# The second token tile's residual of the expert layers added by VectorE at the layer's end, in place of two identity products of TensorE in front of the experts

## The reference, cut to what matters

```
h = _layer_norm(DN_ALPHA * h + mix, ln_g[layer, 0], ln_b[layer, 0])
ffn = _grouped_moe(h, w_router, b_router, w_gu[layer], w_down[layer])
h = _layer_norm(DN_ALPHA * h + ffn, ln_g[layer, 1], ln_b[layer, 1])
```

## Time and profile before

| | us |
|---|---|
| median of 3 runs | 666.47 |
| the three runs | 663.47, 667.05, 666.47 |
| the profiled execution | 664.13 |
| its span, first to last instruction | 662.4 |

### The profile page before, as it was taken

The page is one execution under the profiler, slowest core; times in us unless marked ns, Lnnn a source line. Parts: engine busy times, 40 slices in busy tenths (PEclk is TensorE's granted clock), DMA queues, the critical chain, the costliest instruction groups (busy, mean ns, idle before and its releaser), DMA issues.

```text
span 662.4 us, 7170 instructions
## 1 busy us (share of the span) xinstructions
PE 643.2 (97%) x2750; PEld 287.1 (43%) x2750; DVE 293.9 (44%) x774; ACT 146.9 (22%) x331; POOL 18.6 (3%) x37
## 2 busy tenths in 40 slices
PE   6999999999999999999999999999999999999993
PEld 5854564564333333333334455556333333333331
DVE  0010303467435345254365346668444434435356
ACT  1030343231121121121222042333112021021122
POOL 2030200000000000000000000100000000000000
PEclk9999999999999999999999999999999999999998
DMA  8999926266999999999999980946999999999981
GB/s 302 387 404 348 425 114 229 88 223 232 421 421 421 421 421 422 421 421 421 421 416 413 421 366 25 368 149 240 409 410 420 422 421 419 422 421 421 420 363 64
DMA packets 41448, 231.43 MB, mean 349 GB/s; under 512 B 10170, under 2 KB 10170, under 8 KB 15811
## 3 DMA queue, kind: packets, MB, share of 16 engines
q1 hardware_dynamic: 36976, 230.72, 85.8%
q10 hardware_dynamic: 4434, 0.21, 0.5%
HBM read 229.87 MB, written 1.05 MB: 349 GB/s over the span
## 4 chain that ended last, share of the span: by engine, by line
PE 94%; DVE 3%; DMA 1%; ACT 1%; issue 0%; SPq 0%; DVEq 0%; ACTq 0%
PE pb L679 33%; PE pb L478 20%; PE pb L709 16%; PE pb L537 5%; PE pb L729 4%; PE pb L851 2%; PE pb L652 2%; PE pb L435 1%; PE pb L428 1%; PE pb L631 1%; PE pb L654 1%; PE pb L446 1%; DVE bufC L1466 1%; DMA ring<-in_w_in_a 1%; PE pb L891 1%; PE pb L595 1%
## 5 line engine op out<-in xcount | busy, mean ns | idle before, releaser
L478 PE MATMUL pb<-ring,hT 128*128 128x512 f32 x320 | 144.4, 597 | 0.1
L709 PE MATMUL pb<-ring,bufC 128*64 128x512 f32 x512 | 116.4, 596 | 0.9 <-DVE bufC L1466 0.9
L679 PE MATMUL pb<-ring,hT 128*64 128x512 f32 x512 | 113.5, 593 | 0.0
L679 PE MATMUL pb<-ring,bufB 128*64 128x512 f32 x480 | 106.4, 593 | 0.0
L1466 DVE STREAM_TRANSPOSE bufC<-bufC 32x128 f32<-32x128 f32 x256 | 103.0, 402 | 3.8
L1492 DVE COPY bufA<-pb 32x512 f32<-32x512 f32 x64 | 43.7, 682 | 118.1 <-PE pb L709 117.0
L478 PEld LDWEIGHTS pb<-ring,hT 128*128 128x128 f32 x320 | 58.4, 190 | 64.5 <-issue 62.5
L679 PEld LDWEIGHTS pb<-ring,hT 128*64 128x64 f32 x512 | 36.4, 137 | 71.5 <-issue 71.5
L709 PEld LDWEIGHTS pb<-ring,bufC 128*64 128x64 f32 x512 | 34.8, 137 | 68.1 <-issue 65.3
L679 PEld LDWEIGHTS pb<-ring,bufB 128*64 128x64 f32 x480 | 33.9, 137 | 67.2 <-issue 65.4
L1069 ACT ACTIVATE bufA<-pb 32x512 f32<-32x512 f32 x64 | 37.8, 590 | 111.1 <-PE pb L709 110.3
(11 more groups left out here) (246 smaller groups left out, 430.3 us busy)
## 6 DMA issues: line engine op xcount, KB each, us to landing
ring<-in_w_gu SPq DMA_DIRECT2D x124, 1024.0 KB, 20.9
ring<-in_w_down SPq DMA_DIRECT2D x64, 1024.0 KB, 20.4
ring<-in_w_in_a SPq DMA_DIRECT2D x11, 1024.0 KB, 18.5
ring<-in_w_out_a SPq DMA_DIRECT2D x4, 1024.0 KB, 20.9
ring<-in_w_q_b SPq DMA_DIRECT2D x4, 1024.0 KB, 23.2
ring<-in_w_out_b SPq DMA_DIRECT2D x4, 1024.0 KB, 24.2
bufA<-in_w_gu SPq DMA_DIRECT2D x2, 1024.0 KB, 6.1
hT<-in_w_gu SPq DMA_DIRECT2D x2, 1024.0 KB, 7.6
```

The lines of the kernel that those rows point to most:

```text
L478: last = mm(pb[bank][:, :], hT[:, k, t * P:(t + 1) * P], slot(i0 + k // 2)[0][:, k % 2, c * HALF:(c + 1) * HALF], start=k == 0, stop=k == ...
L679: last = mm(pb[0][c * 64:(c + 1) * 64, :].rearrange("p (a n) -> p a n", a=2), xe[m % 2][:, k, g * SLOTS:(g + 1) * SLOTS], w.rearrange("p ( ...
L709: last = mm(to[c * 64:(c + 1) * 64, :], heT[u == EXPERTS - 1][:, (2 * hf + j) * 64:(2 * hf + j + 1) * 64], w[:, j, c * HALF:(c + 1) * HALF ...
```

## The change

The two `seed` products of tile 1 are taken out of each of the two layers, half 0 behind `place(l, 1)` and half 1 behind `gate_up(0)`. The wait on `ln_ready` that stood in front of half 0 stays. Banks 6 and 7 now start with the first scatter of the layer (start=True for t = 1, m = 0). At the end of the layer VectorE computes `ALPHA * h + bank` for each half of tile 1 into `res`, waits for it (`link`), takes `bn_stats` from `res`, and reads `res` again in the step of line 1560. Tile 0 is as it was.

```diff
-                def seed(t, c):
+                def seed(c):
-                    pe.wait_ge(ln_ready, 2 * (2 * NT * l + t) + c + 1)
-                    mm(pb[4 + 2 * t + c][:, :], alpha_i[:, :], h[:, t, c * HALF:(c + 1) * HALF],
+                    pe.wait_ge(ln_ready, 2 * 2 * NT * l + c + 1)
+                    mm(pb[4 + c][:, :], alpha_i[:, :], h[:, 0, c * HALF:(c + 1) * HALF],
                        start=True, stop=False, skip_group_check=True)
...
-                                     ye[t][:, c * HALF:(c + 1) * HALF], start=False, stop=m == QUADS - 1,
+                                     ye[t][:, c * HALF:(c + 1) * HALF], start=t == 1 and m == 0, stop=m == QUADS - 1,
...
                 place(l, 1)
                 pe.wait_ge(ln_ready, 2 * (2 * NT * l + 1) + 2)
-                seed(1, 0)
                 gather(0, 1, 3)
                 gather(0, 3, 2)
                 gate_up(0)
-                seed(1, 1)
...
                 for c in range(2):
                     dve.wait_ge(mix_done, 4 * n + 2 * t + c + 1)
-                    link(V.bn_stats(ln[:, t, 6 * c:6 * c + 6], pb[4 + 2 * t + c][:, :]))
+                    cc = slice(c * HALF, (c + 1) * HALF)
+                    if t:
+                        link(V.scalar_tensor_tensor(out=res[:, t, cc], in0=h[:, t, cc], scalar=ALPHA,
+                                                    in1=pb[4 + 2 * t + c][:, :], op0=ALU.mult, op1=ALU.add))
+                    link(V.bn_stats(ln[:, t, 6 * c:6 * c + 6], res[:, t, cc] if t else pb[4 + c][:, :]))
...
-                    V.scalar_tensor_tensor(out=res[:, t, cc], in0=pb[4 + 2 * t + c][:, :], scalar=ln[:, t, 12:13],
+                    V.scalar_tensor_tensor(out=res[:, t, cc], in0=res[:, t, cc] if t else pb[4 + c][:, :], scalar=ln[:, t, 12:13],
                                            in1=ln_row[0][:, cc], op0=ALU.subtract, op1=ALU.mult)
```

More of the change, by code:

```diff
@@ L744, in moe @@
                 for c in range(2):
-                    seed(0, c)
+                    seed(c)
                 stay_awake(3, 1)
```

## The result

The changed kernel is slower: 669.95 us median (667.55 to 670.85, 13 runs) against 666.19 us (663.47 to 667.05, 13 runs), ratio 1.006 with a 95% interval of 1.0047 to 1.0074. The executions of either kernel fall into two groups some 2 us apart (before 5 around 664.1 and 8 around 666.6 us, changed 6 around 668.4 and 7 around 670.4), and group against group the changed kernel is 4.3 and 3.8 us slower. The profiled execution took 670.52 us, in the upper group; that of the kernel before, 664.13, was in the lower.

A forecast was written before the change was run, and what follows sets the result against it. TensorE's chain of products, 94% of the 662.4 us, bounds the kernel. The terms -0.62 + 1.45 + 1.45 = +2.28 us gave 666.4 us profiled and 668.7 us on the median, 0.34% slower; range 665.5 to 670.9.

The forecast's parts named there:

- rival C: Layer 0's end: longer TensorE idling before the K/V projection lets its clock fall; +4.5 us, time 670.9; chance 0.10.
- Transfers at nothing: Whole kernel: transfers end ahead of their use and shift with TensorE, so they were put at nothing.
- The products, -0.62 us: Tile 1's four removed TensorE products, both layers: half 0 gains 0.31 us per layer, half 1 gains 0; 0.62 in all.
- Rival A: Both layers: the four removed products count in full, 3.44 us gained, giving -0.54 us in all; chance 0.05.
- The additions, 1.45 us at each end: Both layers' ends: VectorE's two new multiply-adds per layer are paid in full, 1.45 us each end.
- rival B: Layer 0's end: the 1.45 us vanish in VectorE's free time before tile 1's transposition; sum +0.83, 667.3 us; chance 0.11.
- The SBUF source: VectorE's four operations reading SBUF instead of PSUM: rows show at most 2 ns gain, against a page's 65 ns each.
- The clock at nothing: Layer 0's end: the sum has no term for TensorE's clock falling while it idles 2.6 us before the projection.
- C's price: Clock fall at layer 0's end: half speed for 4.4 us, read from the kernel's start, costs 2.2 us.

The follow-up runs named there:

- e4: Against the kernel before, only the two tile 1 products per layer removed, VectorE's layer end as before (residual left out): 663.65 us, ratio 0.9987.
- e1: Changed kernel, but at layer 0's end ScalarE copies transposed tile 0 before taking tile 1's square root: 664.87 us, ratio 1.0005 to the kernel before.
- e2: Changed kernel plus two unread identity products on TensorE behind tile 0's transposition at layer 0's end: 666.54 us, ratio 1.0031 to the kernel before.
- e5: Kernel before with only VectorE's two multiply-adds per layer added, all TensorE products kept: 668.9 us, ratio 1.0076, 6 runs.
- e3: Changed kernel with half 1's product back behind gate and up, VectorE adding only half 0's residual: 667.88 us, ratio 1.0032 to the kernel before.
- e8: Kernel before with ScalarE's copies ahead of the root, half 0's product replacing an identity product, and line 550's four products split in pairs: 663.53 us, ratio 0.9982.

## Why the prediction was right in its range, and which term its sum lacked

The measured 669.95 us lies in the range of 665.5 to 670.9, on the side that was forecast, but beyond the forecast of 668.7 and slower by over 0.5%, to which I gave 0.23. The ends of the forecast's own terms reached only to 669.7: the result is inside because the range was stretched to rival C, to which I gave 0.10. Step by step:

- **Transfers at nothing**: right. From the first product of expert 1 to the start of the last scatter it is 181.95 us in both kernels in layer 0 (347.97 - 166.02 and 345.83 - 163.88).
- **The products, -0.62 us**: measured -0.55 by landmarks and 0.9987 in e4. In layer 0 half 1 gave 0.04 us (forecast 0) and half 0 gave 0.23 (forecast 0.31, ends 0.22 and 0.41): the gather's weight load came 0.12 us behind the table (155.91 - 155.79), where 0.05 us had been seen. Rival A is refuted by e4 and by both idle times.
- **The additions, 1.45 us at each end**: measured 1.43 and 1.44. Reading who is queued behind the square root was the step that counted: rival B, which looks only at tile 1's own users, would have given +0.83 us. e1 shows that another order of ScalarE, in two places, makes it true.
- **The SBUF source**: the rows were right to go by. The 65 ns per operation, estimated from the Trainium skill, "VectorE: DVE Perf Modes", section "The TRN2 errata — SBUF-src ops pay a fixed extra latency per instruction", did not show: with the source in SBUF `bn_stats` is 4 ns shorter and the step behind it 3 ns longer.
- **The clock at nothing is the step that failed.** The sum has no term for it; it stood only in rival C, and C is what happened. The trace of the changed kernel shows it, e2 and e5 tie it to the idle stretch, and the times say that it happens in all 13 runs: the lowest is 667.55 us, and the eight lower runs of e2, in which the clock stays up, lie from 666.26 to 666.61. The sentence that misled me is "An idle stretch of 2.6 us is shorter than that, which speaks against C". I took the 4.4 us between the last product and the fall at the kernel's end as a time that idling must last. But that fall shows only that 4.4 us are enough: I used an upper bound as a lower one. In the changed kernel the clock fell 2.2 us after the last product (356.04 to 358.2), before the projection had started.
- **C's price**, 2.2 us, was too high: 1.48 us in the trace, 1.70 in e5's, 1.9 from the medians of e2. I took it from the kernel's start, where half speed for 4.4 us was my own reading: the granted clock in both stretches of the earlier trace rows is 1.00. In layer 0's end the clock was low for 3.4 us, and TensorE had work in 3.0 of them.
- **Small slips**: on the highest run of before the forecast is 667.05 + 2.28 = 669.3 us, not 669.4.

Sum: -0.55 + 1.43 + 1.46 + 1.44 = +3.8 us. The forecast of +2.28 lacked the third term, the clock.

## What to carry to other kernels

A product that stands in front of a wait is filler; before moving its work to another engine, read who released the next instruction, and try first to put it where the engine waits anyway. When an engine gets more to do, follow each semaphore it sets to the engine that waits, and then read what is queued behind that wait: here nothing that reads the additions' result was late, but two copies queued behind a square root were. And count the idle time that a delay adds to TensorE: here 1.4 us more of it let the clock fall, which cost as much again. Put the next independent work into it, or, as in e2, two products that nobody reads.

## What the runs showed of the hardware that I had not expected

The granted clock falls after much less than the 4.4 us seen at the end of the kernel. In the two traces with 2.56 and 2.57 us of idle time (changed kernel, e5) it fell 2.2 and 2.8 us after the last product and was then at 1.2 GHz for 3.4 us, although TensorE was soon working again. With 1.85 us of idle time (e3) the one trace has no fall, and only the times speak for one in part of the executions. With 1.14 us or less (kernel before, e4, e1, e2) no trace has one in this place.

And TensorE need not be idle. In four of ten traces the clock fell at the end of four products that multiply over 4 of 128 rows (67.6 to 68.1 us; 2 us by the records, no gap), for 3.4 us and at a price of 1.7 us; the same products are in five traces without a fall. Split in two pairs with full products between (e8), they left none of 12 runs in the upper group, where 14 of 29 runs of the kernel before were.
